# Decoder layer on one core: the products with W_o for the first 128 tokens ordered by kind, and the low parts of W_o cut later

## The chip, the cores and the metric

The kernel runs on 1 core of one Trainium2 chip. The metric is the device time of one execution in microseconds, as the median of the runs. The kernel takes all inputs in float32 and writes a float32 output.

## The reference

One decoder layer over 256 tokens of width 1024. The part that matters here is the end of the token mixer, and what follows it:

```python
merged = g_sb * (o_sb @ w_proj_sb) + g_mb * (o_mb @ w_proj_moba) + g_ds * (o_ds @ w_proj_dsa)
y = merged @ w_o
x = x + g1 * rms_norm(y, g_post_mix[l])
h = rms_norm(x, g_pre_ffn[l]) * (1.0 + sc2) + sh2
gate, up = jnp.split(h @ w_up, 2, axis=-1)
y = (silu(gate) * up) @ w_down
x = x + g2 * rms_norm(y, g_post_ffn[l])
```

Here `o_sb`, `o_mb` and `o_ds` are the outputs of three attention branches, and `g_sb`, `g_mb`, `g_ds` are sigmoid gates by channel.

## The kernel before

**Products in two parts.** A float32 number is cut into a high part (type fp32r, made by a copy on ACT, the scalar engine) and a low part (the rest, a subtraction on DVE, the vector engine). A product a·b is then three products on PE, the tensor engine: high·high, high·low and low·high (`three`, L1577 to L1581). This holds for weights and for activations. DVE can make a low part only after ACT has made the high part.

**The stages around the change.** PE first makes the three branch projections, one 128-channel tile f after another (f = 0 to 7), 25 products a tile. For each tile DVE multiplies by the gates (`gate_tile`, L1409, 128x768), adds the three branches (`merge_two`, L1415, `merge_third`, L1420), and after ACT's copy (`merge_hi`, L974) subtracts for the low part (`merge_lo`, L1425). `merge_lo` of tile f stands behind `merge_two` of tile f + 1. The result is `hhi` and `hlo` (both in the tile `hcut`), the stationary operand of the products with W_o. W_o comes in 8 row blocks k = 0 to 7 of 128x1024. ACT cuts each block's high part (`cut_wo_hi`, L763) and DVE its low part (`cut_wo_lo`, L1119) in the order `WO_ORDER` = 3, 7, 0, 1, 2, 4, 5, 6. Blocks 3 and 7 are cut earlier than this stage. Tables say behind which tile f a block is cut: `WO_HI_AT` for ACT, `WO_LO_AT` (L246) for DVE. Semaphores `wo_hi_done` and `wo_lo_done` count the cut blocks in that order. The raw blocks 0 to 3 lie in the buffer `raw1`, the blocks 4 to 6 in `raw0`.

**The products with W_o** (L1908 to L1936) run over t = 0, 1 (128 tokens each), two column halves n = 0, 1 of 512, and k = 0 to 7, three products each, 48 products for one t. For t = 0 they begin a block k only when its high part, its low part and the tile k's low part are there:

```python
def chunk_ready(k):
    pe.wait_ge(wo_hi_done, WO_RANK[k])
    pe.wait_ge(wo_lo_done, WO_RANK[k])
    pe.wait_ge(m_lo, k + 1)
```

For k = 0 to 3 both halves n go together. For k = 4 to 7 half 0 is finished first, then half 1. t = 0 accumulates in banks 6 and 7 of PSUM, t = 1 in banks 0 and 1.

**What follows.** For each t ACT squares and sums the halves (`norm_y`, L767), DVE scales y by the gain (L1468), makes the inverse root, adds to x, makes the second inverse root, and scales (L1138 on DVE, L1033 on ACT). PE turns the scaled tile over (`turn_x`, L1674), ACT and DVE each modulate half of it (`modulate`, L784 and L1144), and PE makes the first block of the feed-forward with w_up straight from the raw weights (`first_up_0`, `first_up_1`, L1941, 32 products each). `turn_x(0)` stands between the last two twelves of t = 1's products. `first_up_0` waits for all eight modulated pieces of t = 0 (four on `h_act`, four on `h_dve`).

**w_up's second block.** ACT and DVE cut it in four quarters (`second_up_hi`, L993, and `second_up_lo`, L1457). On both engines the quarters stand in the same queue as the work above. On ACT the order is

```python
scale_new_x(0)
second_up_hi(0)     # waits for the block to have landed in raw0
norm_y(0, 1)        # between its halves: modulate(0), second_up_hi(1)
norm_new_x(1)
```

On DVE `second_up_lo(0)` comes ahead of t = 1's gain and `modulate(0)`, and `second_up_lo(1)` behind it.

**The loads** are issued by SP, the sync engine, in program order (L606 to L614):

```python
for i in range(2):
    sp.wait_ge(wo_hi_done, max(WO_RANK[4 * i + kk] for kk in range(4)))
    sp.wait_ge(wo_lo_done, max(WO_RANK[4 * i + kk] for kk in range(4)))
    load_up(i, 1 - i)
```

followed by `load_down(i)`. `load_up(0)` writes w_up's first block (two transfers of 1024 KB, L600) over the raw blocks 0 to 3 of W_o in `raw1`, so it waits for five high and five low parts, that is up to block 2 in `WO_ORDER`. `load_up(1)` writes w_up's second block into `raw0` and waits for all eight. `load_down` is one transfer of 1024 KB (L604). All go through one queue.

Of the kernel before, what the change touches and what calls it, by code (L numbers as in the profile page):

```python
# [25 lines left out]
P = 128  # L26
D = 1024
KC = D // P
S = 256
TT = S // P  # L30
# [12 lines left out]
BANK = 512  # L43
# [84 lines left out]
N_UNITS = len(UNITS)  # L128
# [113 lines left out]
WO_ORDER = [3, 7, 0, 1, 2, 4, 5, 6]  # L242
WO_RANK = {k: n + 1 for n, k in enumerate(WO_ORDER)}
WO_AT = {N_UNITS - 2: [3], N_UNITS - 1: [7]}
WO_HI_AT = {5: [0, 1], 6: [2, 4], 7: [5]}
WO_LO_AT = {5: [0, 1], 6: [2]}  # L246

VEC_GATE, VEC_ADA, VEC_PRE_MIX, VEC_POST_MIX, VEC_PRE_FFN, VEC_POST_FFN, VEC_END = (
    0, 3 * KC, 9 * KC, 10 * KC, 11 * KC, 12 * KC, 13 * KC)
# [25 lines left out]
def decoder_layer(nc, x, c, w_ada, b_ada, g_pre_mix, g_post_mix, w_in, b_gate, w_proj_sb,  # L275
                  w_proj_moba, w_proj_dsa, w_o, g_pre_ffn, g_post_ffn, w_up, w_down, out):
    ctx = ExitStack()
    with ctx:
# [222 lines left out]
        def wo_hi(k):  # L501

            if k == 7:
                return wo_last[:, 0, :]
            if k in (4, 5):
                return wo_early[:, k - 4, :]
            return block_view(whi[(B_WO + k // 4) % 2], B_WO)[:, k % 4, :]

        def wo_lo(k):

            return wo_last[:, 1, :] if k == 7 else block_view(wlo[(B_WO + k // 4) % 2], B_WO)[:, k % 4, :]
# [583 lines left out]
        def _(dve):  # L1095
# [20 lines left out]
            def cut_wo_lo(k):  # L1116

                dve.wait_ge(wo_hi_done, WO_RANK[k])
                dve.tensor_tensor(wo_lo(k), wo_raw(k), wo_hi(k).bitcast(F32), ALU.subtract).then_inc(wo_lo_done, 1)  # L1119
# [302 lines left out]
            def merge_lo(f):  # L1422

                dve.wait_ge(m_hi, f + 1)
                dve.tensor_tensor(hlo[:, f, :], h32[:, f, :], hhi[:, f, :].bitcast(F32), ALU.subtract).then_inc(m_lo, 1)  # L1425
# [18 lines left out]
                    cut_wo_lo(k)  # L1444
            gate_tile(KC - 1)
            merge_two(KC - 1)
            cut_wo_lo(4)
            merge_third(KC - 1)
            merge_lo(KC - 2)
            cut_wo_lo(5)  # L1450
            merge_lo(KC - 1)
            cut_wo_lo(6)

            def second_up_lo(q):

# [120 lines left out]
        def _(pe):  # L1576
# [91 lines left out]
            def turn_x(t):  # L1668

                for half, ready in enumerate((xn_ready, xn_other)):  # L1670
                    pe.wait_ge(ready, t + 1)
                    for c in range(4 * half, 4 * half + 4):
                        dst = bank[B_TURNED[t] + half][:, P * (c % 4):P * (c % 4 + 1)]
                        mm = pe.transpose(dst, xn[:, t, P * c:P * (c + 1)], ident[:, :])  # L1674
                    mm.then_inc(x_turned, 1)
# [172 lines left out]
            k = KC - 1  # L1848
# [59 lines left out]
            def out_part(t, half, n, kk):  # L1908

                k, cols = 4 * half + kk, slice(BANK * n, BANK * (n + 1))  # L1910
                return three(bank[B_Y[0][t] + n][:, :], [x[:, k, P * t:P * (t + 1)] for x in (hhi, hlo)],
                             [wo_hi(k)[:, cols], wo_lo(k)[:, cols]], k == 0, k == KC - 1)

            def chunk_ready(k):

                pe.wait_ge(wo_hi_done, WO_RANK[k])
                pe.wait_ge(wo_lo_done, WO_RANK[k])
                pe.wait_ge(m_lo, k + 1)

            for t in range(TT):  # L1920
                if t == 1:
                    pe.wait_ge(unit_read, N_UNITS)
                for kk in range(4):
                    if t == 0:
                        chunk_ready(kk)
                    for n in range(2):
                        mm = out_part(t, 0, n, kk)
                mm.then_inc(units, 1)
                for n in range(2):
                    for kk in range(4):  # L1930
                        if t == 0 and n == 0:
                            chunk_ready(4 + kk)
                        mm = out_part(t, 1, n, kk)
                    mm.then_inc(units, 1)
                    if t == 1 and n == 0:
                        turn_x(0)  # L1936

            def first_product(t, j, a, k, first, last):

# [136 lines left out]
```

## Time and profile before

| | us |
|---|---|
| median of 3 runs (455.49 to 456.88) | 456.05 |
| the profiled execution | 456.04 |
| its span, first to last instruction | 454.3 |
| PE busy (97% of the span) | 439.9 |
| DVE busy (73%) | 330.7 |
| ACT busy (54%) | 243.7 |
| mean granted clock of PE | 0.997 |

The span is measured by the profiler from the first to the last instruction, so 1.7 us of the execution lie outside it. Busy times are the union of an engine's instructions. PE's matmuls overlap each other in the record, so their starts tell the pace and not their durations. In the views, an idle time in brackets is the engine's idle time just before the row, with what released it. Times are from the span's start.

### The profile page before, as it was taken

What the parts mean: (1) busy time and instruction counts of PE and PEld (TensorE: products, weight loads), DVE (VectorE), ACT (ScalarE), POOL (GpSimd) and SP (SyncE); (2) the same over time, 40 slices, a digit from 0 to 9 for tenths busy, and PEclk for the clock granted to TensorE, in tenths of its full rate; (3) what the DMA queues carried; (4) which work ended last, traced back from release to release, by engine and by line L of the source; (5) the groups of instructions that cost most, each with busy time, mean ns of one, the idle gap of its engine ahead of it and who ended that gap; (6) DMA issues with size and microseconds to landing.
All of it is one profiled execution on the core that took longest, in us unless ns stands there. A gap on an engine that the chain in (4) does not pass through costs nothing.

```text
span 454.3 us, 7880 instructions
## 1 busy us (share of the span) xinstructions
PE 439.9 (97%) x2966; PEld 388.9 (86%) x2966; DVE 330.7 (73%) x587; ACT 243.7 (54%) x432; POOL 34.8 (8%) x76
## 2 busy tenths in 40 slices
PE   4999999999999999999999999999999999999994
PEld 3678988999999899989997899888888888888883
DVE  4625668787998887956995785796696687678655
ACT  4424884556777656596553686533534525425332
POOL 2000102000322231000000001000000000000000
PEclk9999999999999999999999999999999999999998
DMA  8999466886788658746659526988648657530002
GB/s 288 383 378 345 153 231 222 280 297 236 241 302 291 188 180 283 235 150 202 195 200 365 186 68 184 378 302 277 228 159 269 218 190 272 185 138 0 1 0 92
DMA packets 61634, 99.86 MB, mean 220 GB/s; under 512 B 3892, under 2 KB 44452, under 8 KB 61604
## 3 DMA queue, kind: packets, MB, share of 16 engines
q1 hardware_dynamic: 56480, 81.57, 53.2%
q0 software_dynamic: 4960, 17.84, 11.5%
q8 instruction: 19, 0.31, 0.3%
q14 instruction: 11, 0.09, 0.1%
q10 hardware_dynamic: 164, 0.05, 0.0%
HBM read 98.40 MB, written 1.05 MB: 219 GB/s over the span
## 4 chain that ended last, share of the span: by engine, by line
PE 94%; DVE 2%; DMA 1%; issue 1%; ACT 1%; SPq 0%; DVEq 0%; ACTq 0%
PE psum L1579 17%; PE psum L1994 16%; PE psum L1580 16%; PE psum L1581 16%; PE psum L1995 8%; PE psum L1641 7%; PE psum L1941 3%; PE psum L1595 2%; PE psum L1768 1%; DVE wlo L1113 1%; DMA xt<-in_x_dram 1%; PE psum L1703 1%; PE psum L1701 1%; PE psum L1630 1%; PE psum L1750 1%
## 5 line engine op out<-in xcount | busy, mean ns | idle before, releaser
L1994 PE MATMUL psum<-hcut,whi 128*128 128x512 f32 x320 | 111.7, 392 | 0.0
L1995 PE MATMUL psum<-hcut,wlo 128*128 128x256 f32 x320 | 89.6, 280 | 0.0
L1579 PE MATMUL psum<-hcut,whi 128*128 128x256 f32 x280 | 82.1, 293 | 0.3 <-DVE wlo L1113 0.3
L1580 PE MATMUL psum<-hcut,whi 128*128 128x256 f32 x280 | 79.1, 283 | 0.0
L1581 PE MATMUL psum<-hcut,wlo 128*128 128x256 f32 x280 | 79.1, 282 | 0.0
L1113 DVE TENSOR_TENSOR wlo<-raw,whi 128x768 fp32r<-128x768 f32 (+3 forms) x68 | 64.4, 973 | 15.3 <-ACT whi L749 14.7
L1994 PEld LDWEIGHTS psum<-hcut,whi 128*128 128x128 f32 x320 | 59.9, 187 | 13.3
L1995 PEld LDWEIGHTS psum<-hcut,wlo 128*128 128x128 f32 x320 | 60.5, 189 | 0.3
L749 ACT ACTIVATE whi<-raw 128x768 fp32r<-128x768 f32 (+3 forms) x68 | 55.6, 850 | 6.8 <-PE psum L1905 3.2
L1579 PEld LDWEIGHTS psum<-hcut,whi 128*128 128x128 f32 x280 | 53.4, 191 | 5.5 <-ACT qk L829 2.0
L1580 PEld LDWEIGHTS psum<-hcut,whi 128*128 128x128 f32 x280 | 53.5, 191 | 0.0
L1581 PEld LDWEIGHTS psum<-hcut,wlo 128*128 128x128 f32 x280 | 53.5, 191 | 0.0
L1490 DVE TENSOR_TENSOR dlo<-draw,dhi 128x2048 fp32r<-128x2048 f32 x11 | 25.1, 2292 | 35.6 <-ACT dhi L1008 35.6
L1485 DVE TENSOR_TENSOR wlo<-raw,whi 128x1024 fp32r<-128x1024 f32 x36 | 42.4, 1220 | 3.0 <-ACT whi L1001 3.0
L1057 ACT ACTIVATE fsil<-fsil 128x256 f32<-128x256 f32 x20 | 8.4, 418 | 63.5 <-DVE fsil L1504 63.5
L1001 ACT ACTIVATE whi<-raw 128x1024 fp32r<-128x1024 f32 x36 | 35.9, 1045 | 0.0
L1580 PE MATMUL psum<-dlo,fhi 128*128 128x512 f32 x88 | 34.4, 391 | 0.0
L1579 PE MATMUL psum<-dhi,fhi 128*128 128x512 f32 x88 | 34.4, 391 | 0.0
L1581 PE MATMUL psum<-dhi,flo 128*128 128x512 f32 x88 | 34.2, 389 | 0.0
L1008 ACT ACTIVATE dhi<-draw 128x2048 fp32r<-128x2048 f32 x11 | 21.0, 1915 | 22.5 <-PE psum L1581 22.5
L1184 DVE SCALAR_TENSOR_TENSOR acc<-xn,csil,acc 128x1024 f32<-128x1024 f32 x21 | 26.9, 1282 | 4.6 <-DMA xn<-in_w_ada_dram 4.1
L1580 PE MATMUL psum<-wlo,hcut 128*128 128x320 f32 (+2 forms) x76 | 26.2, 345 | 0.0
(252 smaller groups left out, 817.3 us busy)
## 6 DMA issues: line engine op xcount, KB each, us to landing
raw<-in_w_up_dram SPq DMA_DIRECT2D x22, 1024.0 KB, 7.6
xn<-in_w_ada_dram POOLq DMA_DIRECT2D x32, 512.0 KB, 4.9
raw<-in_w_in_dram SPq DMA_DIRECT2D x6, 2048.0 KB, 9.0
draw<-in_w_down_dram SPq DMA_DIRECT2D x11, 1024.0 KB, 5.0
ada<-in_w_ada_dram SPq DMA_DIRECT2D x16, 384.0 KB, 9.2
raw<-in_w_in_dram SPq DMA_DIRECT2D x3, 1536.0 KB, 8.9
raw<-in_w_o_dram SPq DMA_DIRECT2D x8, 512.0 KB, 4.6
raw<-in_w_in_dram SPq DMA_DIRECT2D x3, 1280.0 KB, 7.0
```

The lines of the kernel that those rows point to most:

```text
L749: act.activation(block_view(whi[b % 2], b)[0:p, chunks, cols], block_view(raw[b % 2], b)[0:p, chunks, cols], ACT.Copy).then_inc(w_hi, 1)
L1001: act.activation(block_view(whi[part], B_FFN)[:, 2 * q:2 * q + 2, :], block_view(raw[part], B_FFN)[:, 2 * q:2 * q + 2, :], ACT.Copy).then_ ...
L1113: dve.tensor_tensor(block_view(wlo[b % 2], b)[0:p, chunks, cols], block_view(raw[b % 2], b)[0:p, chunks, cols], block_view(whi[b % 2], b)[ ...
L1184: ins = dve.scalar_tensor_tensor(sums, part, csil[:, k:k + 1], sums, ALU.mult, ALU.add)
L1485: dve.tensor_tensor(block_view(wlo[part], B_FFN)[:, 2 * q:2 * q + 2, :], block_view(raw[part], B_FFN)[:, 2 * q:2 * q + 2, :], block_view(w ...
L1490: dve.tensor_tensor(dlo[slot][:, :, :], draw[slot][:, :, :], dhi[slot][:, :, :].bitcast(F32), ALU.subtract).then_inc(d_lo, 1)
L1579: pe.matmul(dst, a[0], b[0], start=first, stop=False)
L1580: pe.matmul(dst, a[0], b[1], start=False, stop=False)
L1581: return pe.matmul(dst, a[1], b[0], start=False, stop=last)
L1641: mm = pe.matmul(first_place(u)[0:n, :], w, h[:, k, :], start=k == 0 and i == 0 and u in (1, 2, 4, 6, 8), stop=k == KC - 1 and i == 2, ski ...
L1994: pe.matmul(dst[:, :], wh, hcut[:, k, :, :].rearrange("p a s -> p (a s)"), start=k == 0, stop=False)
L1995: mm = pe.matmul(dst[:, S:2 * S], wl, hhi[:, k, :], start=False, stop=k == KC - 1)
```

## The change

Three things. First, PE's products for t = 0 go by kind: for k = 0 to 7 the high part of W_o's block with `hhi` and then with `hlo`, for both halves n (32 products, L1921 of the changed kernel), and then, for half 0 and then half 1, `hhi` with the low parts in `WO_ORDER` (8 products each, L1927). The wait for a low part of W_o stands only at the latter, at half 0. Second, DVE cuts fewer low parts of W_o between the merges: block 0 behind tile 6's `gate_tile`, block 1 behind the last `merge_third`, and blocks 2, 4, 5 and 6 after the last `merge_lo`. Third, `merge_lo` of tile 6 comes ahead of `merge_third` of tile 7. The products for t = 1, the engines ACT, SP and POOL and the waits of SP are the same.

```diff
--- before.py
+++ after.py
@@ -243,7 +243,7 @@
 WO_RANK = {k: n + 1 for n, k in enumerate(WO_ORDER)}
 WO_AT = {N_UNITS - 2: [3], N_UNITS - 1: [7]}
 WO_HI_AT = {5: [0, 1], 6: [2, 4], 7: [5]}
-WO_LO_AT = {5: [0, 1], 6: [2]}
+WO_LO_AT = {6: [0]}
 
 VEC_GATE, VEC_ADA, VEC_PRE_MIX, VEC_POST_MIX, VEC_PRE_FFN, VEC_POST_FFN, VEC_END = (
     0, 3 * KC, 9 * KC, 10 * KC, 11 * KC, 12 * KC, 13 * KC)
@@ -1444,12 +1444,12 @@
                     cut_wo_lo(k)
             gate_tile(KC - 1)
             merge_two(KC - 1)
-            cut_wo_lo(4)
+            merge_lo(KC - 2)
             merge_third(KC - 1)
-            merge_lo(KC - 2)
-            cut_wo_lo(5)
+            cut_wo_lo(1)
             merge_lo(KC - 1)
-            cut_wo_lo(6)
+            for k in (2, 4, 5, 6):
+                cut_wo_lo(k)
 
             def second_up_lo(q):
 
@@ -1911,29 +1911,38 @@
                 return three(bank[B_Y[0][t] + n][:, :], [x[:, k, P * t:P * (t + 1)] for x in (hhi, hlo)],
                              [wo_hi(k)[:, cols], wo_lo(k)[:, cols]], k == 0, k == KC - 1)
 
-            def chunk_ready(k):
-
-                pe.wait_ge(wo_hi_done, WO_RANK[k])
-                pe.wait_ge(wo_lo_done, WO_RANK[k])
-                pe.wait_ge(m_lo, k + 1)
-
-            for t in range(TT):
-                if t == 1:
-                    pe.wait_ge(unit_read, N_UNITS)
+            def out_by_kind():
+
+                for k in range(KC):
+                    pe.wait_ge(wo_hi_done, WO_RANK[k])
+                    for i, (x, ready) in enumerate(((hhi, m_hi), (hlo, m_lo))):
+                        pe.wait_ge(ready, k + 1)
+                        for n in range(2):
+                            pe.matmul(bank[B_Y[0][0] + n][:, :], x[:, k, 0:P], wo_hi(k)[:, BANK * n:BANK * (n + 1)],
+                                      start=k == 0 and i == 0, stop=False)
+                for n in range(2):
+                    for i, k in enumerate(WO_ORDER):
+                        if n == 0:
+                            pe.wait_ge(wo_lo_done, WO_RANK[k])
+                        mm = pe.matmul(bank[B_Y[0][0] + n][:, :], hhi[:, k, 0:P], wo_lo(k)[:, BANK * n:BANK * (n + 1)],
+                                       start=False, stop=i == KC - 1)
+                    if n == 0:
+                        mm.then_inc(units, 2)
+                    else:
+                        mm.then_inc(units, 1)
+
+            out_by_kind()
+            pe.wait_ge(unit_read, N_UNITS)
+            for kk in range(4):
+                for n in range(2):
+                    mm = out_part(1, 0, n, kk)
+            mm.then_inc(units, 1)
+            for n in range(2):
                 for kk in range(4):
-                    if t == 0:
-                        chunk_ready(kk)
-                    for n in range(2):
-                        mm = out_part(t, 0, n, kk)
+                    mm = out_part(1, 1, n, kk)
                 mm.then_inc(units, 1)
-                for n in range(2):
-                    for kk in range(4):
-                        if t == 0 and n == 0:
-                            chunk_ready(4 + kk)
-                        mm = out_part(t, 1, n, kk)
-                    mm.then_inc(units, 1)
-                    if t == 1 and n == 0:
-                        turn_x(0)
+                if n == 0:
+                    turn_x(0)
 
             def first_product(t, j, a, k, first, last):
 
```

The DVE queue before, from the cut of W_o's block 0 on (`wlo1<-raw1,whi1` is a cut of block 0, 1 or 2; `prod<-psum,qk` is `gate_tile`, the two after it are `merge_two` and `merge_lo`, `xn<-prod` is `merge_third`):

```order
L1119 TENSOR_TENSOR wlo1<-raw1,whi1 128x1024
L1415 TENSOR_TENSOR prod1<-prod1 128x256
L1425 TENSOR_TENSOR hcut<-xn,hcut 128x256
L1420 TENSOR_TENSOR xn<-prod1 128x256
L1119 TENSOR_TENSOR wlo1<-raw1,whi1 128x1024
L1409 TENSOR_TENSOR prod0<-psum,qk 128x768
L1119 TENSOR_TENSOR wlo1<-raw1,whi1 128x1024
```

The same place in the changed kernel, from the `gate_tile` of tile 6 on:

```order
L1409 TENSOR_TENSOR prod0<-psum,qk 128x768
L1119 TENSOR_TENSOR wlo1<-raw1,whi1 128x1024
L1415 TENSOR_TENSOR prod0<-prod0 128x256
L1425 TENSOR_TENSOR hcut<-xn,hcut 128x256
L1420 TENSOR_TENSOR xn<-prod0 128x256
L1409 TENSOR_TENSOR prod1<-psum,qk 128x768
L1415 TENSOR_TENSOR prod1<-prod1 128x256
L1425 TENSOR_TENSOR hcut<-xn,hcut 128x256
L1420 TENSOR_TENSOR xn<-prod1 128x256
L1119 TENSOR_TENSOR wlo1<-raw1,whi1 128x1024
L1425 TENSOR_TENSOR hcut<-xn,hcut 128x256
L1119 TENSOR_TENSOR wlo1<-raw1,whi1 128x1024
```

The three cuts of blocks 0, 1 and 2 stood around the `gate_tile` of tile 6. Now block 0's is behind that tile, block 1's behind the `merge_third` of tile 7, and block 2's behind the last `merge_lo`.

The PE queue before, at the third block k with its semaphores (L1579, L1580 and L1581 are high·high, `hhi` with the low part, `hlo` with the high part):

```order
L1579 MATMUL psum<-whi,hcut 128x512 [waits m_lo,wo_lo_done,wo_hi_done]
L1580 MATMUL psum<-wlo,hcut 128x512
L1581 MATMUL psum<-whi,hcut 128x512
L1579 MATMUL psum<-whi,hcut 128x512
L1580 MATMUL psum<-wlo,hcut 128x512
L1581 MATMUL psum<-whi,hcut 128x512
```

The PE queue for t = 0 in the changed kernel, whole, with buffers' numbers:

```order
+L1921 MATMUL psum<-whi1,hcut 128x512 x16
+L1921 MATMUL psum<-wo_early,hcut 128x512 x8
+L1921 MATMUL psum<-whi0,hcut 128x512 x4
+L1921 MATMUL psum<-wo_last,hcut 128x512 x4
+L1927 MATMUL psum<-wlo1,hcut 128x512
+L1927 MATMUL psum<-wo_last,hcut 128x512
+L1927 MATMUL psum<-wlo1,hcut 128x512 x3
+L1927 MATMUL psum<-wlo0,hcut 128x512 x3
+L1927 MATMUL psum<-wlo1,hcut 128x512
+L1927 MATMUL psum<-wo_last,hcut 128x512
+L1927 MATMUL psum<-wlo1,hcut 128x512 x3
+L1927 MATMUL psum<-wlo0,hcut 128x512 x3
```

The products that read `wlo` stood one in three, and a group began with waits for all parts. Now the 16 that read low parts stand behind the 32 that read high parts.

The SP queue at the loads of w_up and w_down, the same in both kernels:

```order
L600 DMA raw<-in_w_up_dram 128x8x256 [waits wo_lo_done,wo_hi_done]
L600 DMA raw<-in_w_up_dram 128x8x256
L604 DMA draw<-in_w_down_dram 128x2x1024 [waits merged,units]
L600 DMA raw<-in_w_up_dram 128x8x256 [waits wo_lo_done,wo_hi_done]
L600 DMA raw<-in_w_up_dram 128x8x256
L604 DMA draw<-in_w_down_dram 128x2x1024
```

Its order and its waits did not move. The third row from the last begins w_up's second block; everything stands behind the first wait.

## Rows read from the trace of the kernel before

**Rows 1.** The page, chain that ended last: share of the span by engine.
```profile
PE 94%; DVE 2%; DMA 1%; issue 1%; ACT 1%; SPq 0%; DVEq 0%; ACTq 0%
```
**Rows 2.** Timeline of PE, 232 to 260 us: start, duration, engine, line, tiles, idle before.
```profile
232.71 0.28 PE L1905 MATMUL psum<-ohi,wlo 128*128 128x256 f32 x1
...
235.77 0.39 PE L1579 MATMUL psum<-whi,hcut 128*128 128x512 f32 x1
...
243.71 0.47 PE L1579 MATMUL psum<-whi,hcut 128*128 128x512 f32 x1 [0.53 <-issue]
...
247.97 0.40 PE L1579 MATMUL psum<-whi,hcut 128*128 128x512 f32 x1
...
253.46 0.40 PE L1579 MATMUL psum<-wo_early,hcut 128*128 128x512 f32 x1
...
259.93 2.28 PE L1941 MATMUL psum<-xn,raw 128*128 128x128 f32 x19
```
**Rows 3.** Timeline of DVE, 230 to 243 us.
```profile
230.64 0.94 DVE L1409 TENSOR_TENSOR prod<-psum,qk 128x768 f32<-128x768 f32 x1
...
233.65 1.21 DVE L1119 TENSOR_TENSOR wlo<-raw,whi 128x1024 fp32r<-128x1024 f32 x1
234.78 0.94 DVE L1409 TENSOR_TENSOR prod<-psum,qk 128x768 f32<-128x768 f32 x1
235.65 1.20 DVE L1119 TENSOR_TENSOR wlo<-raw,whi 128x1024 fp32r<-128x1024 f32 x1
...
242.05 0.42 DVE L1425 TENSOR_TENSOR hcut<-xn,hcut 128x256 fp32r<-128x256 f32 x1
242.38 1.22 DVE L1119 TENSOR_TENSOR wlo<-raw,whi 128x1024 fp32r<-128x1024 f32 x1
```
**Rows 4.** SP's row L608: its wait in total, times, longest; its instructions' starts.
```profile
SPq L608 <- DVE wlo L1119: 8.3, 2, 5.8
...
L608 SPq EVENT_SEMAPHORE  x2: 17/17/17, 236.9 to 243.6; - x2
```
**Rows 5.** Stretches: length; busy PE, PEld, DVE, ACT, POOL; PEclk; DMA share; GB/s.
```profile
239.00:255.00 16.00, 15.35 (x66) 11.98 (x65) 9.54 (x22) 6.34 (x18) 0.00 (x0) 1.00 1.08 371
255.00:258.00 3.00, 3.00 (x19) 2.55 (x18) 2.00 (x3) 2.51 (x6) 0.00 (x0) 1.00 0.17 68
```
**Rows 6.** Timeline of ACT, 254 to 260 us.
```profile
254.91 1.06 ACT L993 ACTIVATE whi<-raw 128x1024 fp32r<-128x1024 f32 x1 [0.27 <-DMA raw<-in_w_up_dram]
256.46 0.60 ACT L767 ACTIVATE flo<-psum 128x512 fp32r<-128x512 f32 x1 [0.49 <-PE psum L1581]
...
257.05 1.50 ACT L784 ACTIVATE xn<-psum,col 128x128 f32<-128x128 f32 x4
258.42 1.07 ACT L993 ACTIVATE whi<-raw 128x1024 fp32r<-128x1024 f32 x1
```
**Rows 7.** Timeline of DVE, 256 to 266 us.
```profile
256.00 1.23 DVE L1457 TENSOR_TENSOR wlo<-raw,whi 128x1024 fp32r<-128x1024 f32 x1 [1.54 <-ACT whi L993]
...
257.79 1.36 DVE L1144 TENSOR_SCALAR xn<-psum,col 128x128 f32<-128x128 f32 x4
259.53 1.23 DVE L1457 TENSOR_TENSOR wlo<-raw,whi 128x1024 fp32r<-128x1024 f32 x1 [0.38 <-ACT whi L993]
...
265.94 0.48 DVE L1138 TENSOR_SCALAR xn<-xt,rinv 128x512 f32<-128x512 f32 x1
```
**Rows 8.** The chain of work that ended last, in order of time: start, duration, work.
```profile
267.24 0.45 PE psum L1674 x4
267.71 0.47 ACT xn L784
268.22 7.56 PE psum L1941 x64
...
447.94 0.24 PE psum L1581
```
**Rows 9.** Stretches, the same columns as in rows 5, at the span's end.
```profile
451.00:452.00 1.00, 0.00 (x0) 0.00 (x0) 0.84 (x2) 0.00 (x0) 0.00 (x0) 0.69 0.00 0
```

## The prediction

> **What bounds the kernel now.** I read the chain of waits first: 94% of it is PE's own work [rows 1]. So time goes down only where PE stands still, and any new idle time of PE is paid in full, since nothing after it on PE is short of work. Then I read PE's timeline around the change. The 48 products of t = 0 run from 235.77 to 247.97, which is 12.20 us. The first 24 of t = 1 run from 247.97 to 253.46, 0.229 us each [rows 2]. At that pace 48 products take 10.98 us, so t = 0 loses 1.2 us. PE stood idle for 0.53 us ahead of the product at 243.71 [rows 2], and the rest is short waits of the same kind around it. DVE's timeline says for what: the last cut of W_o starts at 242.38 and lasts 1.22 us, so it ends at 243.60, just ahead of 243.71 [rows 3]. PE waits there for low parts, as the change assumes.
>
> Then I asked who else waits for those low parts. SP does, at L608: it waited for the low parts twice, and its instructions there stand at 236.9 and 243.6 [rows 4]. These release w_up's first block (at 236.9, when the cut that began at 235.65 and lasts 1.20 has ended [rows 3]) and w_up's second block. From 239 to 255 the DMA engines are full: share 1.08 at 371 GB/s, and 0.17 after that [rows 5]. ACT waited 0.27 us for the second block of w_up and began to cut it at 254.91 [rows 6]. So that block came in at the end of a queue that ran without a gap since it was released at 236.9, and it was already the last thing that ACT waited for.
>
> **The change, part by part.**
>
> *PE's order for t = 0.* As many products of the same shape, so no work is added. Without waits they take 48 x 0.229 = 11.0 us and end at 246.8 in place of 247.97, a gain of 1.2 us up to that point. Do waits come back? The 32 products with high parts take until 235.77 + 7.3 = 243.1; ACT's order is unchanged, and PE comes to tile 7 only at 242.2, which ACT cuts in about 1 us after its last merge. The low part of the last block is wanted 7 products later, at 244.7.
>
> *DVE's order.* I lay the new queue out from `gate_tile` of tile 6. DVE gets there at 230.64 + 0.87 + 3 x 0.33 = 232.5 and now must wait for tile 6's last product, which starts at 232.71 and lasts 0.28: 233.0 [rows 2, 3]. Before, a cut of W_o filled this. Steps by their spacing: 0.87 for a gate (234.78 to 235.65), 1.13 for a cut (233.65 to 234.78), 0.33 for a 128x256 (242.05 to 242.38) [rows 3]. Up to the cut of block 2 there are two gates, two cuts and seven small ones: 1.74 + 2.26 + 2.31 = 6.3, so it starts at 239.3 to 239.4 and ends 1.2 later; with 0.1 us for each of two hand-overs to DVE, at 240.7. Blocks 4, 5 and 6 follow at 1.13 each, so the last ends at 244.1. PE wants it at 244.7, with 0.6 to spare. The other low parts are earlier still. So PE's gain stands.
>
> *SP's wait.* Here is the cost. L608's first wait needs five low parts, up to block 2. Before it ended at 236.85 [rows 3], now at 240.7: w_up's first block is released 3.8 us later. w_down's first block and w_up's second stand behind it in the same queue, and the engines had no idle time to make this up in [rows 5]. The wait for w_up's second block (eight low parts, 243.6 before, 244.1 now) moves little, but its data are behind 3 MB that start 3.8 us later. So I take its landing as 254.9 + 3.8 = 258.7.
>
> The least that this delay can be I take from the trace too: five transfers of the six, 5.24 MB, at 371 GB/s from 239 on end by 253.1, while ACT got the block at 254.9 [rows 5, 6]. It was 1.8 us later than its place in line, next to the last transfer. If that part went away, the landing would be 2.0 us later and not 3.8. The upper end is 4.3, if 0.5 us of the second release is added. I take 3.8, since nothing in the order of the last two transfers changes.
>
> A rule bears on this sentence. The Trainium skill, DMA: Bandwidth & Descriptors, "Queues, rings and completion order", says that one engine's descriptors are consumed in ring order but that completion is not first in, first out. By strict ring order the block would be there by 253.1, and the sum below would end at +1.6; the trace, with 254.9, shows the later completion.
>
> *What is late next.* ACT stands at `second_up_hi(0)` until 258.7. Behind it are t = 1's square sum (0.6 us), `modulate(0)` (1.50 us) and the second quarter's cut, in order, with nothing to overtake [rows 6]. Before, the square sum itself waited 0.49 us for PE; that wait disappears. So from ACT's cut to `modulate(0)`: 258.7 + 1.0 + 0.6 = 260.3 and its end at 261.8; the second quarter from 261.7 (1.37 after `modulate(0)` starts, 257.05 to 258.42). On DVE the first quarter's low part starts 1.09 after ACT's, 259.8, `modulate(0)` 1.79 later at 261.6, done at 262.9, and the second quarter's low part at 262.8 to 262.9, against 259.53 before [rows 7]. That is +3.4, which is the 3.8 less 0.4 for the wait that is gone.
>
> PE ends t = 1 at 259.93 - 1.2 = 258.7 [rows 2]. Then it must wait until 261.8 for `h_act`, a new idle time of 3.1 us. `first_up_0` takes 267.24 - 259.93 = 7.3 us [rows 2, 8], to 269.1. DVE's chain from the second quarter on (inverse roots, x, scale) took 6.4 us, 259.53 to 265.94 [rows 7]; it now gives the scaled tile at 269.3. Before, PE already waited behind this chain for `modulate(1)`: the chain of waits goes PE, ACT, PE at 267.24, 267.71, 268.22 [rows 8]. So `first_up_1` starts at 268.22 + 3.4 = 271.6. From there on PE has work to the end in both kernels, and its loads move with the same chain, so nothing gives the 3.4 us back.
>
> **Sum:** PE's stalls of 1.2 us go, but what they gained turns into part of the new wait, since the start of `first_up_1` is set by the late block. Net +3.4 us. The profiled execution took 456.04, the median is 456.05, so the sum can be laid on either: 459.4.
>
> **The rivals.**
>
> *The late block costs nothing (not slower).* If the block's landing were set by its own release, 0.5 us later than before, and not by the 3.8 us of the queue ahead of it, ACT would start at 255.4 and the chain would gain 0.4 and lose 0.5: 456.1. This needs engines with room between 239 and 255; the share of 1.08 over the whole stretch speaks against it [rows 5]. It decides at a delay of 0.4 us: below, the kernel is faster, at best by 0.4 us at no delay (455.6), since the old landing at 254.91 then holds ACT. Even a delay of 1.7 us would still read as no change. A gain of over 0.3% (1.37 us) is more than the 1.2 us that PE lost, so it would need a cause I don't see. A measurement of this kernel can tell about 0.3% from no change.
>
> *Landing by place in line.* The delay is 2.0 us, net +1.6: 457.6.
>
> *PE's clock falls in the new idle time.* At the end of the span PE's last product starts at 447.94 and lasts under 0.4 us [rows 8], and in the stretch 451 to 452 the granted clock is 0.69 [rows 9], a mean of its full level (2.4 GHz) and half (1.2 GHz): it fell at 451.4, some 3.1 us after PE had stopped. The new idle time is 3.1 us, so it is at the edge. If it falls, `first_up_0` starts at half clock. If all its 7.3 us ran so, it would cost 7.3, less 0.5 of slack before the scaled tile. No row shows products at half clock, so I bound it by 0 and 6.8, and take 2 us, nearer the lower end, since the work that follows is dense: 461.4.
>
> For this the Trainium skill, TensorE: Matmul & The Clock Gate, Part 1, says that the clock returns to half after a stretch without work and comes back only after sustained work; the trace agrees with the fall, and no stretch here shows the return.
>
> **How the numbers follow.** Late block in full: 0.70, 459.4, its own range 458.8 to 460.2 (delay 3.3 to 4.3). Place in line: 0.10, 457.6. Clock: 0.08, 461.4. No cost: 0.09, 455.6 to 456.3. Something else that is faster: 0.03. The range 457.4 to 461.4 leaves out the cases without cost and the clock's upper half, about 0.16. Slower by over 0.3% (above 457.4): 0.86. Within 0.3%: 0.10. Faster by over 0.3%: 0.04.
>
> **What would show it.** Right: PE's t = 0 in 11.0 us without idle time; SP's first L608 at about 240.8; DMA share over 1 from about 243 to 259; ACT's first L993 at 258.7 with some 5 us of waiting for `raw`; PE idle by 3 us ahead of L1941's counterpart; from there all rows 3.4 later. Wrong: ACT's first cut of w_up near 255, or no idle time of PE behind t = 1. A wait of PE at its low products would mean that DVE's queue is longer than I made it; up to 3 us of that would hide in the new wait.

## The result, and the profile after

The changed kernel is slower: 457.73 us (median of 11 runs, 456.95 to 458.93) against 455.96 us for the kernel before (11 runs, 454.91 to 456.93). The ratio is 1.0044, with a 95% interval of 1.0035 to 1.0053, so +1.6 to +2.4 us where +3.4 was forecast. The sign and the mechanism were right, and the size was not. The time lies inside the stated range of 457.4 to 461.4, 0.3 us above its lower bound, and below the range of the main case by itself (458.8 to 460.2).

| profiled execution | before | after |
|---|---|---|
| its time | 456.04 | 456.95 |
| span | 454.3 | 455.2 |
| PE busy | 439.9 | 439.3 |
| DVE busy | 330.7 | 330.5 |
| ACT busy | 243.7 | 243.4 |
| mean granted clock of PE | 0.997 | 0.997 |

These two executions differ by 0.91 us, less than the medians do. The reason lies upstream of the change: the profiled execution of the changed kernel reached its first product with `h` (L1641) at 17.58, the other at 18.54, and so came to PE's first product with W_o at 234.72 in place of 235.77. Laid on each other at that product, which I call S from here on, they differ by 0.91 + 1.05 = 1.96 us. All comparisons of a moment below are made from S.

PE's timeline of the changed kernel:

```profile
234.72 3.82 PE L1921 MATMUL psum<-whi,hcut 128*128 128x512 f32 x16
...
242.08 0.39 PE L1927 MATMUL psum<-wlo,hcut 128*128 128x512 f32 x1
...
245.77 0.39 PE L1579 MATMUL psum<-whi,hcut 128*128 128x512 f32 x1
...
257.45 0.39 PE L1581 MATMUL psum<-wo_last,hcut 128*128 128x512 f32 x1
...
259.60 7.59 PE L1950 MATMUL psum<-xn,raw 128*128 128x128 f32 x64 [1.75 <-ACT xn L784]
...
268.94 7.75 PE L1950 MATMUL psum<-xn,raw 128*128 128x128 f32 x64 [0.46 <-ACT xn L784]
...
276.45 0.48 PE L2003 MATMUL psum<-hcut,whi 128*128 128x512 f32 x1
```

No row of t = 0 has an idle time: the 48 products take 245.77 - 234.72 = 11.05 us, against 12.20 [rows 2]. Then, behind t = 1, stands an idle time of 1.75 us that the kernel before did not have, and ACT's `modulate` ended it.

What came late is in the timelines of DVE and SP, and in SP's row of its wait:

```profile
238.46 1.22 DVE L1119 TENSOR_TENSOR wlo<-raw,whi 128x1024 fp32r<-128x1024 f32 x1
239.60 2.35 DVE L1119 TENSOR_TENSOR wlo<-raw,wo_early 128x1024 fp32r<-128x1024 f32 x2
241.87 1.22 DVE L1119 TENSOR_TENSOR wlo<-raw,whi 128x1024 fp32r<-128x1024 f32 x1
```
```profile
SPq L608 <- DVE wlo L1119: 10.9, 2, 9.7
...
L608 SPq EVENT_SEMAPHORE  x2: 17/17/17, 239.7 to 243.1; - x2
```
```profile
239.75 1.00 SPq L600 DMA_DIRECT2D raw<-in_w_up_dram  x2
240.85 1.02 SPq L604 DMA_DIRECT2D draw<-in_w_down_dram  x1
...
243.16 3.89 SPq L600 DMA_DIRECT2D raw<-in_w_up_dram  x2
```

The low part of block 2 is the cut that starts at 238.46 and ends at 239.68. SP's first wait ends there, 5.03 us after S; before it ended 1.16 after S (236.93, [rows 4]). So w_up's first block was released 3.87 us later, as forecast (3.8). The last low part ends at 243.09, in time for PE.

ACT's timeline shows what that did:

```profile
256.42 1.06 ACT L993 ACTIVATE whi<-raw 128x1024 fp32r<-128x1024 f32 x1 [3.97 <-DMA raw<-in_w_up_dram]
257.38 0.58 ACT L767 ACTIVATE flo<-psum 128x512 fp32r<-128x512 f32 x1
257.95 1.50 ACT L784 ACTIVATE xn<-psum,col 128x128 f32<-128x128 f32 x4
259.33 1.07 ACT L993 ACTIVATE whi<-raw 128x1024 fp32r<-128x1024 f32 x1
```

ACT stood 3.97 us for w_up's second block, and 0.27 before [rows 6]. With it waited the square sum, `modulate(0)` and the second quarter. But it began at 256.42, which is 21.70 after S, where the kernel before began at 254.91, 19.14 after S: 2.56 us later and not 3.8. This is nearly the whole of my error, and the chain of waits runs through it. Its rows of after, by time:

```profile
238.54 4.55 DVE wlo L1119 x4
243.16 0.37 SPq L600
243.57 12.82 DMA raw<-in_w_up_dram
256.42 1.07 ACT whi L993
```

The chain enters at the block's own release by the four last low parts (243.16), which is only 0.5 us later after S than before (8.43 and 7.91). The 12.82 us of transfer hold the time behind the 3 MB ahead of it, and these are what the first release set going late. The transfer of the second block is on the chain that ended last; before, DMA had 1% of that chain and PE 94% [rows 1], and now the shares read `PE 84%; DVE 6%; DMA 5%; ACT 2%`. (Part of that is upstream, where the chain took another of two near-equal ways: `w_ada`'s transfers have 2%.)

The DMA engines were as full as before [rows 5] from the first release on, and the work moved as a whole:

```profile
242.00:256.00 14.00, 14.00 (x67) 11.56 (x66) 6.02 (x16) 4.08 (x13) 0.00 (x0) 1.00 1.08 366
```

The arithmetic from S closes. The release moves by +3.87. From that release to ACT's cut it was 254.91 - 236.93 = 17.98 us before and is 256.42 - 239.75 = 16.67 now, -1.31. So ACT's cut moves by +2.56. From ACT's first quarter to its second it was 3.51 us before (22.65 less 19.14 after S) and is 2.91 now, -0.60, the wait for PE that the square sum no longer has. That is +1.96, the whole difference of the two profiled executions. PE begins `first_up_1` only 1.77 later (the table below), but waits for single pieces within it, and its next product (276.45, in the kernel before 275.54) is 1.96 later after S. What had to be found out is the 1.31.

### The profile page after: what moved, and what is told of

It is laid out like the page before. It is cut to its first block, busy times and chain, and to the rows that moved or that the text cites. A ratio compares the mean times of both kernels' runs of the same rounds, so it can differ in the third digit from the quotient of the medians.

```text
span 455.2 us, 7881 instructions
## 1 busy us (share of the span) xinstructions
PE 439.3 (97%) x2966; PEld 388.9 (85%) x2966; DVE 330.5 (73%) x587; ACT 243.4 (53%) x432; POOL 35.1 (8%) x76
## 3 DMA queue, kind: packets, MB, share of 16 engines
HBM read 98.40 MB, written 1.05 MB: 218 GB/s over the span
## 4 chain that ended last, share of the span: by engine, by line
PE 84%; DVE 6%; DMA 5%; ACT 2%; SPq 1%; issue 1%; DVEq 0%; ACTq 0%
PE psum L2003 16%; PE psum L1579 15%; PE psum L1580 14%; PE psum L1581 14%; PE psum L2004 8%; PE psum L1641 7%; DMA raw<-in_w_up_dram 3%; DMA ada<-in_w_ada_dram 2%; DVE wlo L1119 1%; PE psum L1950 1%; PE psum L1595 1%; PE psum L1768 1%; DVE wlo L1113 1%; PE psum L1703 1%; PE psum L1701 1%
## 5 line engine op out<-in xcount | busy, mean ns | idle before, releaser
L1579 PE MATMUL psum<-hcut,whi 128*128 128x256 f32 x280 | 82.1, 293 | 0.3 <-DVE wlo L1113 0.3
L1580 PE MATMUL psum<-hcut,whi 128*128 128x256 f32 x280 | 79.1, 283 | 0.0
L1581 PE MATMUL psum<-hcut,wlo 128*128 128x256 f32 x280 | 79.1, 282 | 0.0
L1579 PEld LDWEIGHTS psum<-hcut,whi 128*128 128x128 f32 x280 | 53.4, 191 | 5.5 <-ACT qk L829 2.0
L1580 PEld LDWEIGHTS psum<-hcut,whi 128*128 128x128 f32 x280 | 53.6, 191 | 0.0
L1581 PEld LDWEIGHTS psum<-hcut,wlo 128*128 128x128 f32 x280 | 53.5, 191 | 0.0
L1580 PE MATMUL psum<-dlo,fhi 128*128 128x512 f32 x88 | 34.4, 391 | 0.0
L1579 PE MATMUL psum<-dhi,fhi 128*128 128x512 f32 x88 | 34.4, 391 | 0.0
L1581 PE MATMUL psum<-dhi,flo 128*128 128x512 f32 x88 | 34.2, 389 | 0.0
L672 POOL DMA_DIRECT2D xn<-in_w_ada_dram x24 | 13.0, 541 | 140.8 <-DVE acc L1184 71.9
```

What stands on the lines that cost most here:

```text
L1579: pe.matmul(dst, a[0], b[0], start=first, stop=False)
L1580: pe.matmul(dst, a[0], b[1], start=False, stop=False)
L1581: return pe.matmul(dst, a[1], b[0], start=False, stop=last)
```

## The experiments

Times from S, PE's first product with W_o. "Packet" is the start of a transfer in the DMA queue that the trace calls instruction: 16 KB, about 1.1 us long where it falls among w_up's and w_down's transfers. The trace does not record which of the 16 DMA engines carried it. Each row is read from one profiled execution.

| | release (SP's first L600) | ACT's first quarter (its wait) | release to that | `first_up_0` | `first_up_1` | packet |
|---|---|---|---|---|---|---|
| before | 1.16 | 19.14 (0.27) | 17.98 | 24.16 | 32.45 | 11.1 |
| after | 5.03 | 21.70 (3.97) | 16.67 | 24.88 | 34.22 | 4.4, next 27.6 |
| e1 PE's order alone | 1.15 | 18.67 (0.95) | 17.5 | 22.96 | 31.25 | 1.5 |
| e2 DVE's order alone | 5.03 | 23.26 (3.13) | 18.23 | 26.44 | 35.79 | 12.6 |
| e3 after, w_up ahead | 5.03 | 19.22 (1.51) | 14.2 | 22.96 | 31.74 | 3.8 |
| e4 before, one load held | 1.15 | 19.05 (0.19) | 17.9 | 24.15 | 32.44 | 11.2 |
| e5 after, 270 waits | 5.18 | 23.39 (5.67) | 18.21 | 26.56 | 36.66 | 15.2 |
| e6 PE alone, w_up ahead | 1.16 | 17.59 (none) | - | 22.93 | 31.22 | 8.6 |
| e7 after, quarter later | 5.03 | 21.82 (0.24) | 16.8 | 22.96 | 32.48 | 0.8 |
| e8 before, 170 waits | 1.16 | 18.77 (none) | - | 24.14 | 32.43 | none |

The kernel before ran at 455.85 us (29 runs) beside e1, e2, e3 and e4, and at 455.75 us (23 runs) beside the others.

**e1: PE's new order with DVE's old one.** Against the changed kernel:

```diff
-WO_LO_AT = {6: [0]}
+WO_LO_AT = {5: [0, 1], 6: [2]}
...
-            merge_lo(KC - 2)
+            cut_wo_lo(4)
             merge_third(KC - 1)
-            cut_wo_lo(1)
+            merge_lo(KC - 2)
+            cut_wo_lo(5)
             merge_lo(KC - 1)
-            for k in (2, 4, 5, 6):
-                cut_wo_lo(k)
+            cut_wo_lo(6)
```

> PE's order by kind alone; DVE cuts W_o's low parts in the old places. Theory 1 (the cost is the late release of w_up's first block by SP's wait for the low part of W_o's block 2): SP's first L608 stands again 1.2 us after PE's first product with W_o, ACT's first cut of w_up about 19.1 us after that product (21.7 in the changed kernel), PE keeps its 48 products of t = 0 in 11.1 us, and the time is 0.4 us under the kernel before, about 455.6. Rival (the order by kind on PE, or what it does to the chain of ACT and DVE behind it, costs by itself): about 1.8 us over before, 457.7.

Measured: 454.87 us (12 runs), ratio 0.9975, interval 0.9959 to 0.9991. PE's half of the change is worth 1 us when DVE keeps its order, and the cost lies wholly in DVE's half. In PE's timeline t = 1 is followed at once by `first_up_0`; in ACT's the wait is under a microsecond:

```profile
258.39 7.31 PE L1950 MATMUL psum<-xn,raw 128*128 128x128 f32 x64
```
```profile
254.10 1.06 ACT L993 ACTIVATE whi<-raw 128x1024 fp32r<-128x1024 f32 x1 [0.95 <-DMA raw<-in_w_up_dram]
```

The gain was larger than the 0.4 us that I expected. In the profiled execution ACT had the block 0.5 us earlier after the release than in the kernel before, and the square sum lost 0.6 us of waiting and not 0.4.

**e2: DVE's new order with PE's old one,** the same lines the other way round, made in the kernel before.

> DVE's new order alone; PE's products as before. Theory 1: the release is 3.8 us late as in the changed kernel, and PE also waits for low parts in t = 0 (about 1.1 us longer than before, 13.3 us), which hides in the wait for the late block: 1.8 to 2.2 us over before, 457.8 to 458.2, the same as the whole change. Rival (PE's stalls and the late block add up): about 3 us over before, 459.

Measured: 459.43 us (6 runs), ratio 1.0062, interval 1.0040 to 1.0084. By the medians this is 1.7 us more than the whole change, from S to the end of the span 1.3 us more (221.8 and 220.5), and more than I had expected. The number is nearer to the rival's 459, but PE's rows below speak against its reason. Whether the halves add up can't be told from the times: the medians give -1.0 and +3.6, together +2.6, the ratios -1.1 and +2.8 (1.8 to 3.8), together +1.7, the profiled executions from S -1.3 and +3.3, together +2.0, where the whole change gives +1.8 to +2.0. PE's rows:

```profile
240.29 0.47 PE L1579 MATMUL psum<-whi,hcut 128*128 128x512 f32 x1 [2.03 <-issue]
...
263.14 7.59 PE L1941 MATMUL psum<-xn,raw 128*128 128x128 f32 x64 [0.86 <-ACT xn L784]
```

PE's stall for the late low parts (2.03 us at 240.29) is not what costs: in this kernel too PE ends by waiting for ACT behind t = 1, so a stall ahead of that is covered. What costs is the block. It was released exactly as late as in the changed kernel (5.03) and came 1.56 us later:

```profile
259.96 1.06 ACT L993 ACTIVATE whi<-raw 128x1024 fp32r<-128x1024 f32 x1 [3.13 <-DMA raw<-in_w_up_dram]
```

So here are two kernels with SP's queue and DVE's order alike, and 18.23 and 16.67 us from release to ACT's cut. The kernel before has 17.98. My forecast had assumed that this time is the same in all of them.

**e3: the changed kernel with w_up's second block ahead of w_down's first in SP's queue.**

```diff
                 load_up(i, 1 - i)
-                if i == 0:
-
-                    sp.wait_ge(units, BLOCK_DONE[B_WO - 1])
-                    sp.wait_ge(merged, KC)
+            sp.wait_ge(units, BLOCK_DONE[B_WO - 1])
+            sp.wait_ge(merged, KC)
+            for i in range(2):
                 load_down(i, 1 - i)
```

> The whole change, but SP loads both blocks of w_up ahead of both blocks of w_down. Theory 1: w_up's second block has 1 MB less ahead of it, 2.8 us at 371 GB/s, so ACT's first cut of it starts about 18.9 us after PE's first product with W_o; the idle time of PE behind t = 1 is gone or under 0.5 us; 0.4 to 1.2 us under before, 454.8 to 455.6. Rival (it is not this block that PE waits for): no change from the changed kernel, 457.7.

Measured: 455.20 us (12 runs), ratio 0.9983, interval 0.9969 to 0.9997, as expected. When the block that ACT waits for has 1 MB less ahead of it, the excess of the change is gone. It is the landing of this block that carries the loss. The late low parts still cost a little: ACT waits 1.51 us for the block, and `first_up_1` starts at 31.74, where e1 and e6, with DVE's old order, have 31.25 and 31.22.

**e7: the changed kernel with the first quarter's cut behind `modulate(0)`,** on ACT and on DVE, so that a late block holds up nothing that does not need it.

```diff
                     if k == 0 and t == 1 and n == 0:
                         modulate(0)
+                        second_up_hi(0)
                         second_up_hi(1)
...
             scale_new_x(0)
-            second_up_hi(0)
             norm_y(0, 1)
...
                     modulate(0)
+                    second_up_lo(0)
                     second_up_lo(1)
...
-                for q in ((0,), (2, 3))[t]:
+                for q in ((), (2, 3))[t]:
```

> The changed kernel, but on ACT and DVE the cut of the first quarter of w_up's second block stands behind modulate(0), next to the second quarter, so that a late block holds up nobody that PE waits for. Theory 1 (the cost is paid because modulate(0) stands behind a cut that waits for the late block): the block lands as late as in the changed kernel, PE has no idle time behind t = 1 and the time is within 0.4 us of before, 455.7 to 456.4. Rival (PE would wait for something else behind t = 1, or the two quarters in a row delay t = 1's own chain as much): 457 or more.

Measured: 456.15 us (12 runs), ratio 1.0011, interval 1.0000 to 1.0022, as expected. The block comes as late as in the changed kernel, but ACT does `modulate(0)` meanwhile, waits 0.24 us in place of 3.97, and PE has no idle time behind t = 1. ACT's timeline, then PE's:

```profile
256.75 1.50 ACT L784 ACTIVATE xn<-psum,col 128x128 f32<-128x128 f32 x4
...
258.49 2.01 ACT L993 ACTIVATE whi<-raw 128x1024 fp32r<-128x1024 f32 x2 [0.24 <-DMA raw<-in_w_up_dram]
```
```profile
259.63 7.31 PE L1951 MATMUL psum<-xn,raw 128*128 128x128 f32 x64
```

So it was the order of the queue behind the late block that turned a late load into idle time of PE. Nothing of PE's 1.2 us is left at `first_up_1`, though (32.48, before 32.45): with both cuts behind `modulate(0)`, the chain that ends there is as late as it was.

**e6: e1 with w_up ahead as in e3.**

> PE's order by kind, DVE's cuts in the old places, and SP loads both blocks of w_up ahead of w_down's. Theory 1: w_up's second block is there before ACT asks for it (17.9 us after PE's first product with W_o), ACT no longer waits for it, and the whole of PE's 1.2 us comes through: 454.8, at most 0.2 us under PE's order alone. Rival (something else in the chain of ACT and DVE holds the end): no change from PE's order alone, 454.9 to 455.1; if loading w_down later costs anything, more.

Measured: 454.91 us (12 runs), ratio 0.9975, interval 0.9964 to 0.9985. The block's last engine reported 2.0 us earlier than in e1 (16.61 against 18.65), ACT did not wait for it and began 1.1 us earlier, and yet the time is e1's, as the rival had it: with ACT free of that wait, 31.22 against 31.25 at `first_up_1`, another part of the chain holds.

**e4: is the transfer slowed by the one behind it?** In the kernel before, w_down's second block follows w_up's second at once. If the 16 DMA engines divide themselves between the two, the one that was asked for first comes late. Here the second load of w_down waits until w_up's second block has landed and ACT has cut its first quarter:

```diff
                     sp.wait_ge(merged, KC)
+                else:
+                    sp.wait_ge(up_hi, 1)
                 load_down(i, 1 - i)
```

> The kernel before, but w_down's second block is loaded only after ACT has cut the first quarter of w_up's second block, so nothing is queued behind that block. It asks why the block landed 2.0 us after its place in line (5.24 MB moved) in the kernel before and only 0.7 us after it in the changed one. Theory A (it shares the engines with the transfer behind it): it lands about 1.3 to 2 us earlier, 17.2 to 17.8 us after PE's first product with W_o, and ACT no longer waits for it. Theory B (one slow DMA engine of the 16 lags): it lands where it did, 19.1 us after. The time is within 0.3% of before under both, since PE sets the next step of ACT.

Measured: 456.35 us (10 runs), ratio 0.9998, interval 0.9983 to 1.0013, and the landing has not moved, with nothing behind it. The row of w_up's second block (two loads, from issue to landing), of the kernel before and then of e4:

```profile
DMA to landing us min/median/max: 8.2/9.5/10.8
```
```profile
DMA to landing us min/median/max: 8.3/9.5/10.7
```

Sharing falls. What replaces it shows in e4's stretch from 250 to 254. The engines are on average only half busy, with the last part of the block still to come:

```profile
q1 hardware_dynamic: 627, 0.62, 49.4%
```

and in the row of GB/s of that stretch the rate falls to `20 31 20 20 31` from 252 on. A full set of engines moved 371 in [rows 5], so one engine's share is 23: one engine works alone, and the load counts as landed only when it has finished. The trace records, for each of the 16 engines, when it reports its share of the block. From S:

```
             15 engines by    the last    packet at
before           17.83          19.12        11.1
e4               17.74          19.03        11.2
e2               21.58          23.24        12.6
e5               21.81          23.36        15.2
after            21.68          (the 16th with them)   4.4
e7               21.80          (the 16th with them)   0.8
e6               15.89          16.61         8.6
e8               17.82          (the 16th with them)   none
e3               19.20          (the 16th with them)   3.8
e1               spread from 17.33 to 18.65            1.5
```

Fifteen engines moved by 21.68 - 17.83 = 3.85 us between the kernel before and the changed one, which is the delay that I forecast. The sixteenth did not, because in the kernel before it was 1.3 us late. In each kernel in which one engine is late (before, e2, e4, e6 and, below, e5), an instruction packet went over a DMA engine between the release and the landing, and where all sixteen report together it lay ahead of the release or there was none. The moment at which the one engine falls behind fits too: in each of the five all sixteen report together for every load that is done when the packet starts, and one is late from the first or second load on that ends after that. In e6 (packet at 8.6) the load that reports at 9.16 still has all sixteen together, and the next has fifteen by 12.90 and the last at 13.64. In e5 (15.2) all sixteen are there at 13.31, and for the next load fifteen by 15.90 and the last at 17.40. The DMA queues from 239 to 255 of the kernel before, and from 242 to 256 of the changed one, which has no such packet there (queue, kind: packets, MB, share of 16 engines):

```profile
q1 hardware_dynamic: 4480, 5.93, 107.5%
q8 instruction: 1, 0.02, 0.4%
```
```profile
q1 hardware_dynamic: 4221, 5.13, 108.4%
```

The packet's place moves with PE's program, but not with that alone. With PE's old order it stands at 11.1, 11.2 and 12.6 (before, e4, e2). With PE's new order, and no more than the queues of SP, DVE and ACT different, it stands at 0.8, 1.5, 3.8, 4.4 and 8.6 (e7, e1, e3, the changed kernel, e6). To test its part and not argue it, two kernels move the packet by waits that are already met, added at the start of PE's program. They cost time there (S is 10.7 us later than in the changed kernel with 270 of them, and 4.8 later than in the kernel before with 170), and so they are read from S.

**e8: the kernel before with 170 such waits, to take the packet out of the stretch.**

```diff
-            pe.wait_ge(ident_ready, 1)
+            for _ in range(170):
+                pe.wait_ge(ident_ready, 1)
```

> The kernel before with 170 waits on a count that is already there at PE's start. Theory F: the instruction packet that came 11.1 us after PE's first product with W_o comes 2 to 3 us after it or earlier, none lies between 4 and 18, and the second block of w_up lands about 16.6 us after SP's release in place of 18.0, so ACT does not wait for it. The stage is as long as before, since PE's next product sets it. Theory G: it lands 18.0 us after the release.

Measured: 460.57 us in a single run, of which 4.8 lie before S. No packet falls into the transfers, all 16 engines report by 17.82, and ACT no longer waits. The row of w_up's second block, against 8.2/9.5/10.8 before:

```profile
DMA to landing us min/median/max: 6.9/8.2/9.5
```

From its release at 1.16 the block is there 16.7 us later, the changed kernel's 16.67. The kernel is not faster from S on (`first_up_1` at 32.43 against 32.45), since in the old order PE and not the block is late.

**e5: the changed kernel with 270 such waits, to put the packet into the stretch.** The diff is e8's with 270.

> The changed kernel with 270 waits on a count that is already there put at PE's start, where PE waits for x; they make PE's program longer, so that the point at which its next piece is fetched comes earlier in the work. Times are counted from PE's first product with W_o. Theory F (an instruction packet of 16 KB on one of the DMA engines holds that engine up for over 1 us, and a load has landed only when the last engine has ended; the kernel before has one 11.1 us after that product, in the middle of w_up's transfers, the changed kernel has none between 4.4 and 27.6): the packet of 27.6 moves to between 10 and 20, and the second block of w_up lands 17.9 to 18.3 us after SP's release (16.7 in the changed kernel), so that ACT cuts it at about 23.0 and the stage ends 1.3 us later than in the changed kernel. Theory G (the landing differs by chance or by what DVE and PE do meanwhile): 16.7 as in the changed kernel.

Measured: 470.24 us (4 runs), ratio 1.0327, interval 1.0307 to 1.0347, most of it ahead of S. The packet is there at 15.2 and one engine is 1.55 us late. The queues from 253 to 269, then ACT's wait, 5.67 us against 3.97:

```profile
q1 hardware_dynamic: 4366, 5.91, 106.7%
q8 instruction: 1, 0.02, 0.4%
```
```profile
268.79 1.06 ACT L993 ACTIVATE whi<-raw 128x1024 fp32r<-128x1024 f32 x1 [5.67 <-DMA raw<-in_w_up_dram]
```

So 18.21 us from the release, as expected, where 16.67 was without the packet. The stage did not end 1.3 us later than in the changed kernel, as I had expected, but 2.4 (`first_up_1` at 36.66 against 34.22): ACT's cut is 1.69 later, 0.15 of it by the release. Together e8 and e5 give the packet and its absence to both kernels, and each took on the other's transfer time. The rest came with PE's clock. PE's idle time became 3.44 us, and behind it the clock fell from its full level (2.4 GHz) to half (1.2 GHz):

```profile
271.96 9.12 PE L1951 MATMUL psum<-xn,raw 128*128 128x128 f32 x64 [3.44 <-ACT xn L784]
```

with the stretches around it (length; busy PE, PEld, DVE, ACT, POOL; PEclk; DMA share; GB/s):

```profile
271.00:272.00 1.00, 0.04 (x1) 0.07 (x1) 1.00 (x4) 1.00 (x4) 0.00 (x0) 1.00 0.00 0
272.00:273.00 1.00, 1.00 (x8) 0.90 (x8) 1.00 (x5) 1.00 (x2) 0.00 (x0) 0.92 0.00 0
273.00:274.00 1.00, 1.00 (x5) 0.97 (x5) 1.00 (x1) 0.34 (x2) 0.00 (x0) 0.50 0.00 0
...
276.00:277.00 1.00, 1.00 (x9) 1.00 (x9) 1.00 (x2) 0.58 (x2) 0.00 (x0) 0.87 0.00 0
277.00:278.00 1.00, 1.00 (x11) 1.00 (x10) 0.29 (x3) 0.80 (x4) 0.00 (x0) 1.00 0.00 0
```

`first_up_0` took 9.12 us. It takes 7.31 with no wait ahead of it (e1) and 7.59 behind the shorter wait of the changed kernel, so the clock cost 1.5 to 1.8 us there. The stretches at half clock (273 to 276) count 5 to 7 products a microsecond, and the stretch from 277 to 278 at full clock 11. At `first_up_1` 0.75 us of this is left (2.44 less 1.69), since PE had waited there for 0.46 us in the changed kernel.

## Why the prediction was right, and where it was wrong

*PE's order for t = 0: right.* 11.05 us measured, 11.0 forecast, no wait for a low part.

*DVE's order and SP's wait: right.* The low part of block 2 was forecast 3.8 us later, and the release moved by 3.87. That this delay passes through a full set of DMA engines one to one was right too: 15 of the 16 engines moved by 3.85.

*"So I take its landing as 254.9 + 3.8 = 258.7": wrong.* It is the term that was mis-sized: from S, ACT's cut moved by 2.56. The step behind it was "nothing in the order of the last two transfers changes". That holds, but 254.9 was not set by their order. It was set by one engine of 16 that was 1.3 us late, which the runs put down to an instruction packet, and the packet was elsewhere in the changed kernel. Where it would be, the trace of before could not tell. e2 has the same late release with the packet at 12.6, and its time is 459.43, next to the forecast's 459.4. I had the sign of it in the trace: the block was "1.8 us later than its place in line, next to the last transfer". I gave this to the transfer behind it, and e4 shows that it has no part in it.

*Place in line (457.6, given 0.10): the right number for the wrong reason.* Its arithmetic gave +1.6, and the change gave +1.8. Two terms were off and partly made up for each other: a delay of 2.0 less 0.4 for the wait, where 2.56 less 0.60 were measured. It was the case where the late part goes away, and that happened; but the part was not a matter of ring order, and e2 has the same order and lands late. On the rule that I weighed there (the Trainium skill, DMA: Bandwidth & Descriptors, "Queues, rings and completion order"): it leaves the order of completion free, and so decides nothing here. A sentence of the same section bears on what the runs do show, that each engine takes turns between the queues that have work for it, a packet at a time. The trace agrees in so far as one engine alone is late behind the packet, by 1.3 us in the kernel before for a packet of 1.1 us; that this engine carried the packet is argued from the times and not read.

*"The 3.8 less 0.4 for the wait that is gone": too small.* It was 0.60, and the sum is +3.87 - 1.31 - 0.60 = +1.96.

*ACT's queue behind the late block: right.* e7 shows that without it PE does not wait. PE's idle time was 1.75 us and not 3.1, mostly by the 1.31 us above.

*PE's clock (0.08): it did not fall in the changed kernel,* whose new idle time was 1.75 us. In e5 it fell behind an idle time of 3.44 us. This cost 1.5 to 1.8 us on `first_up_0` and 0.75 us at `first_up_1`, where I had taken 2 in all, between bounds of 0 and 6.8. The Trainium skill, TensorE: Matmul & The Clock Gate, Part 1, has the clock return only after sustained work. The trace of e5 agrees: PE worked without a gap from 271.96 on, and the clock was back in the stretch from 276 to 277.

*The late block costs nothing (0.09): wrong,* because the queues in front of it were full, as argued.

The fastest of these kernels are e1 and e6, about 1 us under the kernel before. They keep DVE's order and change PE's (e6 also SP's): PE gets its 1.2 us, and the low parts release SP as early as before.

What stays open. In e1 the 16 engines reported spread out between 17.33 and 18.65, and not fifteen together. Its packet stands at 1.5, just behind the release, and can't by itself make many engines late; I have no cause for this spread, and e1's landing (17.5 us from release to ACT's cut) lies between those with the packet and those without. Nor was it tried what sets the size of the sixteenth's delay, 0.7 us in e6 and 1.7 in e2. Why the packet sits where it does in each kernel is open. Kernels with the same program of PE have it from 0.8 to 8.6 after S, and whether it moves from one execution of a kernel to the next is not known, as each has one profiled execution. That another part of e5 and e8 than the packet moved the landing is not excluded by them alone, as 170 or 270 waits also shift everything by some microseconds; the two act in opposite directions on the same quantity, and e2 agrees without any such waits.

## What to carry to other kernels

Before work is postponed because its next reader can wait, look for its other readers. Here the buffer's release was one, and it came 3.87 us later for the 1.2 us that PE gained. A load that is late costs only what stands behind it in an in-order queue, so put the first use of a late load behind everything that can go ahead of it. And when a transfer lands later than its bytes and the rate allow, ask for the time of each engine and for other queues before laying it on its neighbours.

## What the runs showed of the hardware

- An instruction packet of 16 KB in the middle of a spread load makes it land later, by 0.7 us (e6, packet at 8.6), 1.3 (before, 11.1), 1.7 (e2, 12.6) and 1.55 (e5, 15.2). One engine of 16 reports late, and the load counts when the last has reported. The packet's place is not fixed: it lies from 0.8 to 12.6 after S in the kernels without added waits, and an edit to the queue of SP alone (e1 to e6) goes with a move from 1.5 to 8.6.
- PE's clock fell some 0.9 us after PE had resumed work behind 3.44 us of idle time (0.92 in the stretch from 272 to 273, 0.50 in the next), and not in the idle time itself. It was back within 276 to 277. Behind 1.75 us it did not fall.
- SP's second of two loads in a row took 3.48 us to issue in the changed kernel (`367/1922/3477` for the two of w_up's second block) and 0.58 in the kernel before, where the load behind them took 4.34. It was on nobody's path here, since the engines were full meanwhile.
